# Two of the four down products of each slab of the last MLP, by seven block products in place of eight

## The chip, the cores and the metric

One core of one Trainium2 chip runs the whole program; the metric is its device time in microseconds (us), as the median of three runs. The engines are TensorE (PE in the profile; PEld is its weight load), VectorE (DVE), ScalarE (ACT), GpSimd (POOL) and SyncE (SP), which here only issues DMAs. A difference of about 0.2% of this kernel's time is what a measurement can tell from no change.

## What is computed

A network of four layers on 256 tokens of width 2048, in float32. Only the last part matters here: the second MLP of the second block, and the norm ahead of it and behind it.

```
def sqrelu_mlp(h, w1, w2):
    a = jax.nn.relu(h @ w1)          # 256x2048 @ 2048x8192
    return (a * a) @ w2              # 256x8192 @ 8192x2048

# second_block, last layer (i = 1)
x = x + mix
x = x + sqrelu_mlp(rmsnorm(x, norm_mlp[1]), mlp_w1[1], mlp_w2[1])
return rmsnorm(x, norm_final)
```

Every float32 matrix product is made of three products of a rounded type (fp32r): with a = ah + al and w = wh + wl it is ah·wh + ah·wl + al·wh, summed in PSUM. So each weight is loaded from HBM once, and split on the chip into a high part (a rounding copy) and a low part (the difference).

## The kernel before

**Weights.** SP loads chunks of 512x512 weights (1 MB) into RAW, which has four slots (`NR = 4`, line 18); `load(c)` waits until the chunk that held the slot has been split. A chunk has two halves of 1024 elements a partition. A half is what the rings hold: `split_next` on ACT writes the high part to WH, `split_next` on DVE writes the low part to WL (RAW minus WH), each ring with four places (`RS = 4`). I call a half **a unit**. ACT and DVE run the same loop: during unit n of TensorE they split unit n + 3, and ACT may write its place once TensorE has read unit n - 1.

**The second MLP** (`mlp(1, ...)`, the function `mlp` of each engine) goes over 8 slabs of 1024 hidden columns. One turn of its loop does, for slab s and the slab before: up product `m1u{s}0`, up product `m1u{s}1`, then the four down products `m1d{s-1}0` to `m1d{s-1}3`, each 512 output columns wide. An up product is 8 units: 16 blocks of 128 rows, four column blocks, three matmuls each, 192 matmuls that move 256 columns (tokens) past a 128x128 weight block. A down product is 4 units: 8 blocks of rows, two blocks of tokens, three matmuls each, 48 matmuls that move 512 columns (weights) past a 128x128 block of tokens. Eight slabs have 32 down products.

Behind each up product and each of its two PSUM banks, ACT takes the relu to RE, DVE multiplies relu by relu into SQ, ACT makes the high part Bh and DVE the low part Bl. Behind each down product DVE adds the two banks, times the squared norm factor of the token, to X (`accumulate`). GpSimd has nothing to do in this MLP; its work ends with the layer before.

**The end.** The last down product `m1d73` goes token block by token block (`gemm_by_tokens`), so that the norm of the first 128 tokens runs beside the matmuls of the second; then come the final norm and the stores.

**Names.** G are the four PSUM banks of the products, T the other four; A3h and A3l are the normed input of the MLP, high and low; RB holds the norm factor of each token along a row.

## Time and profile before

| | |
|---|---|
| device time, median of 3 runs | 2880.29 us (2875.42 to 2881.31) |
| span of the profiled execution | 2881.1 us |
| PE busy in the span | 2841.2 us (99%) |
| one turn of the second MLP, 2305.35 to 2392.41 | 87.06 us |
| DVE / ACT busy in it | 49.4 / 38.2 us |
| GpSimd busy in it | 0 us |

The profile is of one execution. A matmul row's duration is the time until its result is out, some 0.28 to 0.39 us, and rows overlap; what a matmul costs TensorE is the distance from start to start. In a timeline a row is the start, the duration, engine, line, operation, out<-in, and behind it in brackets the idle time of the engine ahead of it and what ended that. The chain view gives start, length and work of each piece of the chain that ended last. In a table of windows each engine's busy time stands with its number of instructions, then the granted TensorE clock, the DMA share and GB/s.

### The profile page before, as it was taken

What the parts mean: (1) busy time and instruction counts of PE and PEld (TensorE: products, weight loads), DVE (VectorE), ACT (ScalarE), POOL (GpSimd) and SP (SyncE); (2) the same over time, 40 slices, a digit from 0 to 9 for tenths busy, and PEclk for the clock granted to TensorE, in tenths of its full rate; (3) what the DMA queues carried; (4) which work ended last, traced back from release to release, by engine and by line L of the source; (5) the groups of instructions that cost most, each with busy time, mean ns of one, the idle gap of its engine ahead of it and who ended that gap; (6) DMA issues with size and microseconds to landing.
All of it is one profiled execution on the core that took longest, in us unless ns stands there. A gap on an engine that the chain in (4) does not pass through costs nothing.

```text
span 2881.1 us, 46128 instructions
## 1 busy us (share of the span) xinstructions
PE 2841.2 (99%) x19454; PEld 2585.9 (90%) x19454; DVE 1848.5 (64%) x2543; ACT 1408.0 (49%) x1980; POOL 374.1 (13%) x420
## 2 busy tenths in 40 slices
PE   8999999999999999999999999989999999999998
PEld 8999988998899998999998899878889899988997
DVE  6998655776576665677665666677555555555555
ACT  5434645556555555444444445654545444444444
POOL 0000000000000000007883654122000000000000
PEclk9999999999999999999999999999999999999999
DMA  7555455552555555567776666586655555555553
GB/s 243 191 190 174 137 201 182 190 188 88 175 188 171 171 174 176 191 203 241 237 239 214 237 234 210 200 248 194 199 191 190 194 197 194 190 190 196 197 192 132
DMA packets 288047, 557.99 MB, mean 194 GB/s; under 512 B 25376, under 2 KB 35872, under 8 KB 287584
## 3 DMA queue, kind: packets, MB, share of 16 engines
q1 hardware_dynamic: 275328, 514.49, 54.3%
q0 software_dynamic: 5600, 22.78, 2.0%
q10 hardware_dynamic: 6912, 17.76, 1.8%
q8 instruction: 154, 2.52, 0.4%
q14 instruction: 53, 0.43, 0.0%
HBM read 530.87 MB, written 24.12 MB: 193 GB/s over the span
## 4 chain that ended last, share of the span: by engine, by line
PE 91%; DVE 4%; ACT 2%; DMA 1%; issue 1%; SPq 0%; ACTq 0%; POOL 0%; DVEq 0%
PE G L506 86%; PE T L506 3%; DVE WL L1714 1%; ACT WH L1103 1%; DVE Y L1722 1%; DMA FD<-s_k 1%; PE T L585 1%; DMA s_k<-VAR 1%; DVE XX L1714 0%; PE G L983 0%; ACT L1100 0%; ACT SC_e L1106 0%; DVE ZZ L2374 0%; DVE ST L1795 0%; DVE SC_e L1722 0%
## 5 line engine op out<-in xcount | busy, mean ns | idle before, releaser
L1714 DVE TENSOR_TENSOR WL<-RAW,WH 128x1024 fp32r<-128x1024 f32 (+1 forms) x948 | 1183.1, 1256 | 766.3 <-ACT WH L1103 756.6
L1103 ACT ACTIVATE WH<-RAW 128x1024 fp32r<-128x1024 f32 (+1 forms) x948 | 994.7, 1056 | 1027.7 <-PE G L506 1026.5
L506 PE MATMUL G<-A1h,WH 128*128 128x256 f32 (+1 forms) x2587 | 720.4, 280 | 3.1 <-DVE WL L1714 2.1
L506 PE MATMUL G<-A1l,WH 128*128 128x256 f32 x2560 | 712.9, 278 | 0.0
L506 PE MATMUL G<-A1h,WL 128*128 128x256 f32 x2560 | 711.5, 278 | 0.0
L506 PEld LDWEIGHTS G<-A1h,WH 128*128 128x128 f32 x2587 | 487.3, 189 | 7.0 <-DVE WL L1714 3.1
L506 PEld LDWEIGHTS G<-A1l,WH 128*128 128x128 f32 x2560 | 483.9, 189 | 0.4
L506 PEld LDWEIGHTS G<-A1h,WL 128*128 128x128 f32 x2560 | 482.9, 189 | 0.0
L506 PE MATMUL G<-WH,Bh 128*128 128x512 f32 x1024 | 399.3, 390 | 0.6 <-DVE WL L1714 0.6
L506 PE MATMUL G<-WH,Bl 128*128 128x512 f32 x1024 | 398.5, 389 | 0.0
L506 PE MATMUL G<-WL,Bh 128*128 128x512 f32 x1024 | 398.5, 389 | 0.0
L506 PE MATMUL G<-A3h,WH 128*128 128x256 f32 (+1 forms) x1033 | 283.4, 276 | 0.0
L506 PE MATMUL G<-A3l,WH 128*128 128x256 f32 x1024 | 283.2, 277 | 0.0
L506 PE MATMUL G<-A3h,WL 128*128 128x256 f32 x1024 | 282.7, 276 | 0.0
L506 PEld LDWEIGHTS G<-WH,Bh 128*128 128x128 f32 x1024 | 192.3, 188 | 40.2 <-DVE WL L1714 1.0
L506 PEld LDWEIGHTS G<-WH,Bl 128*128 128x128 f32 x1024 | 192.2, 188 | 40.1
L506 PEld LDWEIGHTS G<-WL,Bh 128*128 128x128 f32 x1024 | 192.3, 188 | 39.0
L506 PE MATMUL G<-WH,A1h 128*128 128x512 f32 (+1 forms) x512 | 203.2, 397 | 0.4 <-DVE WL L1714 0.4
L506 PE MATMUL G<-WH,A1l 128*128 128x512 f32 (+1 forms) x512 | 198.9, 388 | 0.0
L506 PE MATMUL G<-WL,A1h 128*128 128x512 f32 (+1 forms) x512 | 197.6, 386 | 0.0
L506 PEld LDWEIGHTS G<-A3h,WH 128*128 128x128 f32 x1033 | 193.7, 188 | 0.6
L506 PEld LDWEIGHTS G<-A3h,WL 128*128 128x128 f32 x1024 | 192.3, 188 | 0.0
(332 smaller groups left out, 3461.5 us busy)
## 6 DMA issues: line engine op xcount, KB each, us to landing
RAW<-in_mlp_w SPq DMA_DIRECT2D x256, 1024.0 KB, 5.3
RAW<-in_even_w_in SPq DMA_DIRECT2D x52, 1024.0 KB, 5.1
RAW<-in_a_w_in SPq DMA_DIRECT2D x48, 1024.0 KB, 5.2
RAW<-in_b_w_glu SPq DMA_DIRECT2D x32, 1024.0 KB, 5.2
RAW<-in_odd_w_in SPq DMA_DIRECT2D x20, 1024.0 KB, 5.1
RAW<-in_even_w_out SPq DMA_DIRECT2D x16, 1024.0 KB, 5.0
RAW<-in_odd_w_out SPq DMA_DIRECT2D x16, 1024.0 KB, 5.0
RAW<-in_a_w_out SPq DMA_DIRECT2D x16, 1024.0 KB, 5.0
```

The lines of the kernel that those rows point to most:

```text
L506: return e.matmul(out, lhsT, rhs, start=start, stop=stop, skip_group_check=True)
L585: m = e.transpose(T[:, 256 * j + 128 * i:256 * j + 128 * i + 128], X[:, i, c:c + 128], IDENT)
L1103: return e.activation(out, in_, ACT.Copy, scale=scale, bias=0.0)
L1714: return e.tensor_tensor(out, a, b, op)
L1722: return e.scalar_tensor_tensor(out=out, in0=a, scalar=s, in1=b, op0=op0, op1=op1)
```

## The change

**Two of the four down products of a slab** (`SEVEN = (0, 2)`: output columns 0 to 511 and 1024 to 1535) become seven block products. The tokens fall into two halves of 128, the 1024 rows of the slab into two of 512, the 512 columns into two of 256. Eight products of such blocks are the plain way; seven products of sums of blocks give the same. One block product is 4 row blocks by 3 matmuls, 12 matmuls that move 256 columns, and is a unit of the rings: 1024 elements a partition, like a half before. So such a down product has 7 units where it had 4.

**Weight sums on GpSimd:** four adds of 128x1024 for each such down product, S2 = b21 + b22, S1 = b12 + b22, S3 = S1 + b21, S4 = S3 + b11, from the two RAW chunks to TSUM. **Token sums on GpSimd:** four adds of 128x512 a slab, HS to TSUM (named DSUM there). ACT and DVE split them as they split the raw blocks, and the token sums once more to DH and DL.

**The way of the activations:** DVE takes relu times the norm factor to RM in one instruction, ACT squares it to HS; the split of HS to EH and EL, and of the sums to DH and DL, comes as one 128x1024 instruction at each of the first four units of the next up product (`second_highs`, `second_lows`). For the last slab it comes in `m1d62` and `m1d63`. RE, SQ, Bh and Bl fall away. **The sums of products:** seven PSUM halves T are added to ACC in SBUF over all slabs by DVE, and at the end eleven instructions of 128x256 for each of the two turn ACC into X (`add_blocks`). **The order:** up 0, down 0, down 1, up 1, down 2, down 3. **Memory:** the ring's places are 1152 wide for this MLP, WL and others lie elsewhere, GR2 is loaded at the last turn. The norm factor's row RB is made by two more small matmuls in `m1u00`.

The table of the products, and TensorE's part:

```
+SEVEN = (0, 2)
+PRODUCTS = ("21*11", "22*21", "D4*12", "D1*S2", "D2*S1", "D3*S3", "11*S4")
...
+            for q, p in enumerate(PRODUCTS):
+                n = next(half)
+                if q % 2 == 0 and before is not None:
+                    e.wait_ge(*q_acc[before, q // 2])
+                e.wait_ge(*w_lo[n])
+                hi, lo = slot((WH, WHm), n), slot((WL, WLm), n)
+                Ah, Al = blocks(p)
+                o = TB[q // 2][:, 256 * (q % 2):256 * (q % 2) + 256]
+                for j in range(4):
+                    mm(o, Ah[:, j, :], hi[:, j, :], j == 0 and q % 2 == 0, False)
+                    mm(o, Ah[:, j, :], lo[:, j, :], False, False)
+                    m = mm(o, Al[:, j, :], hi[:, j, :], False, j == 3)
+                m.then_inc(*w_read.up(n))
+                step(STEPS[tag])
```

VectorE's part of a down product of seven:

```
+            for h, p in enumerate(PRODUCTS):
+                n = next(half)
+                while split[0] < min(n + RS, limit[0]):
+                    split_next()
+                if h in (2, 4, 6) and not first:
+                    add_products(tag, k, h // 2 - 1)
+                step(STEPS[tag])
+            if not first:
+                add_products(tag, k, 3)
+            if sums:
+                add_blocks(tag, k)
```

GpSimd's weight sums:

```
+            for i in range(2):
+                e.wait_ge(*w_in[(c + i) % NR][c + i])
+            if before is None:
+                e.wait_ge(*x_up["gg3", 1])
+            else:
+                e.wait_ge(*w_lo[product(before, "D2*S1")])
+            tt(S2, b21, b22, ALU.add).then_inc(*t_sum.up((tag, 0)))
+            tt(S1, b12, b22, ALU.add).then_inc(*t_sum.up((tag, 1)))
+            if before is not None:
+                e.wait_ge(*w_lo[product(before, "11*S4")])
+            e.wait_ge(*d_l[s, 1])
+            e.wait_ge(*t_sum[tag, 1])
+            tt(S3, S1, b21, ALU.add).then_inc(*t_sum.up((tag, 2)))
+            e.wait_ge(*t_sum[tag, 2])
+            tt(S4, S3, b11, ALU.add).then_inc(*t_sum.up((tag, 3)))
```

SyncE's wait ahead of a load, for the chunk that held the slot:

```
                 old = c - NR
-                e.wait_ge(*w_lo[half_of[old, 1]])
+                first = old if old in tag_of else old - 1
+                if chunks[old][2]:
+                    tag = tag_of[first]
+                    e.wait_ge(*w_lo[product(tag, "D4*12" if old == first else "22*21")])
+                    e.wait_ge(*t_sum[tag, 3 if old == first else 2])
```

The order of the instructions shows three places. First VectorE, from the first unit of an up product to the end of the down products behind it. Before (an up product's last eight splits, the activations, the first splits of the next product):

```order
L1714 TENSOR_TENSOR WL<-RAW,WH 128x1024 [waits s_w_hi] x8
L1722 SCALAR_TENSOR_TENSOR SQ<-G,RE 128x512 [waits s_m_l,s_m_relu]
L1714 TENSOR_TENSOR Bl<-SQ,Bh 128x512 [waits s_m_h]
L1722 SCALAR_TENSOR_TENSOR SQ<-G,RE 128x512 [waits s_m_l,s_m_relu]
L1714 TENSOR_TENSOR Bl<-SQ,Bh 128x512 [waits s_m_h]
```

Now, for `m1u{s}0` and the product of seven behind it:

```order
L1891 TENSOR_TENSOR WLm<-RAW,WHm 128x1024 [waits s_w_hi]
L1891 TENSOR_TENSOR EL<-HS,EH 128x1024 [waits s_m_h]
L1891 TENSOR_TENSOR WLm<-RAW,WHm 128x1024 [waits s_w_hi]
L1891 TENSOR_TENSOR EL<-HS,EH 128x1024 [waits s_m_h]
L1891 TENSOR_TENSOR WLm<-RAW,WHm 128x1024 [waits s_w_hi]
L1891 TENSOR_TENSOR DL<-TSUM,DH 128x1024 [waits s_d_h]
L1891 TENSOR_TENSOR WLm<-RAW,WHm 128x1024 [waits s_w_hi]
L1891 TENSOR_TENSOR DL<-TSUM,DH 128x1024 [waits s_d_h]
L1891 TENSOR_TENSOR WLm<-RAW,WHm 128x1024 [waits s_w_hi] x4
L1899 SCALAR_TENSOR_TENSOR RM<-G,RB 128x512 [waits s_m_sq,s_bank0]
L1899 SCALAR_TENSOR_TENSOR RM<-G,RB 128x512 [waits s_m_sq,s_w_read]
L1891 TENSOR_TENSOR WLm<-TSUM,WHm 128x1024 [waits s_w_hi] x3
```

Four splits of activations stand among the weights' splits of the up product, and the two RM stand ahead of the split of the fourth block product (the first of the three with TSUM). Second ScalarE at that boundary, now:

```order
L1217 ACTIVATE HS<-RM 128x512 [waits s_d_sum,s_m_l,s_ev_d] x2
L1220 ACTIVATE WHm<-TSUM 128x1024 [waits s_w_read,s_t_sum]
L1220 ACTIVATE EH<-HS 128x1024 [waits s_m_sq,s_w_read]
L1220 ACTIVATE WHm<-TSUM 128x1024 [waits s_w_read,s_t_sum]
L1220 ACTIVATE EH<-HS 128x1024 [waits s_m_sq]
```

The two squares stand ahead of the high part of the fourth block product; here, in `m1d62`, the activations' splits stand among the products too. Third GpSimd, one slab of the MLP, where it had nothing:

```order
L2731 TENSOR_TENSOR TSUM<-HS 128x512 [waits s_w_lo,s_m_sq]
L2731 TENSOR_TENSOR TSUM<-HS 128x512
L2731 TENSOR_TENSOR TSUM<-TSUM,HS 128x512 [waits s_d_sum]
L2731 TENSOR_TENSOR TSUM<-TSUM,HS 128x512 [waits s_p_sum]
L2731 TENSOR_TENSOR TSUM<-RAW 128x1024 [waits s_w_lo,s_w_in3,s_w_in2]
L2731 TENSOR_TENSOR TSUM<-RAW 128x1024
L2731 TENSOR_TENSOR TSUM<-TSUM,RAW 128x1024 [waits s_t_sum,s_d_l,s_w_lo]
L2731 TENSOR_TENSOR TSUM<-TSUM,RAW 128x1024 [waits s_t_sum]
```

Token sums come first, then the four weight sums, the first of which waits for both chunks of the down product and the third for the low part of the token sums; the second down product has the last four rows again.

## Rows read from the trace of the kernel before

**Rows 1.** The page's first part: busy us (share) xinstructions.

```profile
PE 2841.2 (99%) x19454; PEld 2585.9 (90%) x19454; DVE 1848.5 (64%) x2543; ACT 1408.0 (49%) x1980; POOL 374.1 (13%) x420
```

**Rows 2.** Windows: a turn, an up product, a down product.

```profile
2305.35:2392.41 87.06, 87.06 (x578) 79.60 (x577) 49.37 (x49) 38.24 (x40) 0.00 (x0) 1.00 0.58 193
2305.35:2327.12 21.77, 21.77 (x194) 21.77 (x193) 10.98 (x10) 8.87 (x9) 0.00 (x0) 1.00 0.59 191
2348.88:2359.76 10.88, 10.88 (x51) 9.03 (x50) 7.42 (x9) 6.00 (x8) 0.00 (x0) 1.00 0.51 177
```

**Rows 3.** Timeline of PE: an up product's first row.

```profile
2305.35 0.33 PE L506 MATMUL G<-A3h,WH 128*128 128x128 f32 x2
```

**Rows 4.** Timeline of ACT in that turn; columns as above.

```profile
2305.55 1.06 ACT L1103 ACTIVATE WH<-RAW 128x1024 fp32r<-128x1024 f32 x1 [1.60 <-PE G L506]
2308.45 1.06 ACT L1103 ACTIVATE WH<-RAW 128x1024 fp32r<-128x1024 f32 x1 [1.83 <-PE G L506]
2328.64 0.58 ACT L1100 ACTIVATE RE<-G 128x512 f32<-128x512 f32 x1
2330.63 2.00 ACT L1103 ACTIVATE WH<-RAW 128x1024 fp32r<-128x1024 f32 x2
```

**Rows 5.** Timeline of DVE in that turn.

```profile
2306.64 1.23 DVE L1714 TENSOR_TENSOR WL<-RAW,WH 128x1024 fp32r<-128x1024 f32 x1
2329.38 0.68 DVE L1722 SCALAR_TENSOR_TENSOR SQ<-G,RE 128x512 f32<-128x512 f32 x1
2331.71 3.50 DVE L1714 TENSOR_TENSOR WL<-RAW,WH 128x1024 fp32r<-128x1024 f32 x3 [0.26 <-ACT WH L1103]
2359.66 1.41 DVE L1722 SCALAR_TENSOR_TENSOR X<-G,NS,X 128x512 f32<-128x512 f32 x2
```

**Rows 6.** DMA issues: out<-in, engine, count, KB each, median us to landing.

```profile
RAW<-in_mlp_w SPq DMA_DIRECT2D x256, 1024.0 KB, 5.3
```

**Rows 7.** Timelines of POOL and DVE around two long GpSimd operations.

```profile
1762.28 1.91 POOL L2471 TENSOR_TENSOR TC<-CV,ST 128x1024 f32<-128x1024 f32 x1 [3.29 <-issue]
1763.68 1.59 DVE L1714 TENSOR_TENSOR WL<-RAW,WH 128x1024 fp32r<-128x1024 f32 x1 [1.44 <-ACT WH L1103]
1764.14 2.88 POOL L2471 TENSOR_TENSOR TC<-CV,ST 128x1024 f32<-128x1024 f32 x1
...
1779.42 2.39 POOL L2471 TENSOR_TENSOR TS<-TC,TS 128x1024 f32<-128x1024 f32 x1 [7.23 <-ACT TS L1556]
1780.33 2.57 DVE L1714 TENSOR_TENSOR WL<-RAW,WH 128x1024 fp32r<-128x1024 f32 x1 [1.77 <-ACT WH L1103]
```

**Rows 8.** The same where both engines have work queued, 1355 to 1360.

```profile
1355.87 1.66 DVE L1714 TENSOR_TENSOR WL<-RAW,WH 128x1024 fp32r<-128x1024 f32 x1
1356.41 1.62 POOL L2471 TENSOR_TENSOR TS<-TS,LAM 128x256 f32<-128x256 f32 x1
1357.46 1.66 DVE L1714 TENSOR_TENSOR WL<-RAW,WH 128x1024 fp32r<-128x1024 f32 x1
1358.00 1.62 POOL L2471 TENSOR_TENSOR TS<-TS,LAM 128x256 f32<-128x256 f32 x1
```

**Rows 9.** GpSimd's line 2471, duration ns min/median/max.

```profile
L2471 POOL TENSOR_TENSOR TS<-TC,TS x4: 2393/2399/2409, 1779.4 to 1836.5; 128x1024 f32<-128x1024 f32 x4
L2471 POOL TENSOR_TENSOR VAR<-VAR,CV x1: 1050/1050/1050, 1757.9 to 1757.9; 128x512 f32<-128x512 f32 x1
```

**Rows 10.** Timeline of PE behind a wait, and the window of it.

```profile
339.41 0.89 PE L506 MATMUL T<-SC_e,V 128*128 128x256 f32 x4 [1.93 <-ACT SC_e L1103]
341.17 0.41 PE L506 MATMUL G<-A1h,WH 128*128 128x256 f32 x1
341.38 0.41 PE L506 MATMUL G<-A1l,WH 128*128 128x256 f32 x1
340.00:344.00 4.00, 4.00 (x23) 4.00 (x22) 2.75 (x4) 3.36 (x7) 0.00 (x0) 0.57 0.79 262
```

**Rows 11.** Timeline of DVE: the last product's second half of tokens.

```profile
2872.11 0.75 DVE L1722 SCALAR_TENSOR_TENSOR X<-G,NS,X 128x512 f32<-128x512 f32 x1 [1.10 <-PE G L506]
```

More of the change, by code:

```diff
@@ L280, in build_program, with weights @@
     turn = itertools.cycle((0, 2))
-    def weights(tag, w, K, n0, N=512, fm=False, first=0, steps=0, split=True):
+    def weights(tag, w, K, n0, N=512, fm=False, first=0, steps=0, seven=False):
         kts = K // 128
@@ L524, in gemm @@
                     end = seen == kts
-                    hi, lo = WH[:, n % RS, j * N:(j + 1) * N], WL[:, n % RS, j * N:(j + 1) * N]
+                    hi, lo = (slot(ring, n)[:, j * N:(j + 1) * N] for ring in ((WH, WHm), (WL, WLm)))
                     if fm:
@@ L568, in gemm_by_tokens @@
                         e.wait_ge(*w_lo[n])
-                    hi, lo = WH[:, n % RS, j * N:(j + 1) * N], WL[:, n % RS, j * N:(j + 1) * N]
+                    hi, lo = (slot(ring, n)[:, j * N:(j + 1) * N] for ring in ((WH, WHm), (WL, WLm)))
                     mm(o, Ah[:, kt, tk], hi, kt == 0, False)
@@ L1732, in split_next, with gemm @@
             c, h = halves[n]
[L1733 to L1734 removed]
+            if h in PRODUCTS:
+                src = seven_source(tag_of[c], h)
+            else:
+                N = chunks[c][1][1]
+                src = RAW[:, c % NR, h * 2 * N:(h + 1) * 2 * N]
             e.wait_ge(*w_hi[n])
[L1736 to L1739 removed]
+            tt(slot((WL, WLm), n), src, slot((WH, WHm), n).bitcast(F32), ALU.subtract).then_inc(*w_lo.up(n))
+        def gemm(tag, soon=None, at=2):
+            for h in range(units(tag)):
                 n = next(half)
@@ L2218, in dve, with first_mlp @@
         norm_scale("m0", 3)
-        def mlp(l, ph, Ah, Al, gains, after=None):
-            Bh, Bl, RE, SQ = MLP[l]
+        def first_mlp():
             for s in range(9):
@@ new lines, in first_mlp, with second_lows @@
+            finish()
+            norm_scale("s", 3)
+        def second_lows(s):
+            at = s // 7
+            for k in range(2):
+                e.wait_ge(*m_h[1, s, k])
+                low(EL[at][:, 4 * k:4 * k + 4, :], HS[:, 4 * k:4 * k + 4, :], EH[at][:, 4 * k:4 * k + 4, :]).then_inc(
+                    *m_l.up((1, s, k)))
+                yield
+            if at:
+                for _ in range(units("m1d62") - 2):
+                    yield
+            for k in range(2):
+                e.wait_ge(*d_h[s, k])
+                low(DL[at][:, 2 * k:2 * k + 2, :], TSUM[2 + k][:, :].rearrange("p (a b) -> p a b", b=512),
+                    DH[at][:, 2 * k:2 * k + 2, :]).then_inc(*d_l.up((s, k)))
+                yield
```

419 lines of the change are left out of this document (318 added, 101 removed).

## The prediction

> **What bounds the kernel now.** I read the engines' busy time first: TensorE is busy 2841.2 of the span [rows 1]. The windows of one turn of the second MLP come next: TensorE is busy in all of its 87.06 us at a granted clock of 1.00, and VectorE, ScalarE and GpSimd are busy 49.4, 38.2 and 0 us [rows 2]. So what the matmuls cost sets the time, and the other engines matter only where they come too late. The profiled execution's span is 2881.1 us, 0.8 above the median of 2880.29; I work from the span and take the 0.8 off at the end.
>
> How late they may come is in the timelines. An up product starts at 2305.35 [rows 3]. Behind the boundary of a unit ScalarE starts the high part 0.20 later, and 2308.45 is 0.38 behind the next boundary (2305.35 + 2.72); I take 0.33 inside an up product [rows 4]. It takes 1.06, VectorE's low part starts 1.09 after it and takes 1.23 [rows 4, 5]. So a unit's low part is there 2.5 us after the boundary that freed its place, and TensorE wants it three units after that boundary. With units of 2.72 us this is 8.2, a spare of 5.6.
>
> **What the change takes off TensorE.** An up product moves 256 columns in 192 matmuls in 21.77 us, 0.1134 each, with a new weight block each time; a down product moves 512 columns in 48 in 10.88, 0.2267 each [rows 2]. Seven block products are 84 matmuls of 256 columns: 84 x 0.1134 = 9.53. Each replaced product saves 10.88 - 9.53 = 1.36, sixteen save 21.7. The two matmuls for RB cost TensorE about 0.3, by their like of 128 columns.
>
> **What it does to the spare time.** A unit in a product of seven is 12 x 0.1134 = 1.36 us, so three units are 4.08 and the spare is 1.5. And behind an up product it is less. Let 0 be the boundary. VectorE makes RM of the second bank once it is complete (0.33), 0.68 long, 0.69 apart [rows 5]; its end is at about 1.1. ScalarE squares it, 0.58 [rows 4], to 1.7, and only then makes the high part of the fourth block product, for the squares stand ahead of it in its queue: 1.68 to 2.74. VectorE's low part ends at 4.0, and TensorE wants it at 4.08. **The spare of the fourth block product is nil**, and each us by which VectorE comes late to that boundary is a us of waiting. The next ones have little: VectorE needs 1.14 for a split back to back [rows 5] and about 0.71 for each PSUM addition, which the two X of 1.41 show [rows 5], together 2.98 for two products of 2.72; with that the seventh comes just in time (within 0.1). So without GpSimd fourteen of the sixteen pay nothing.
>
> **What GpSimd's sums do to VectorE.** The trace has GpSimd and VectorE's splits side by side, and they shut each other out. GpSimd's 128x1024 addition of two arrays begins at 1779.42 and ends at 1781.81; VectorE's split begins at 1780.33 and takes 2.57 in place of 1.23, that is 1.49 of waiting and 1.08 of work [rows 7]. The other way, GpSimd's second of 1764.14 waits for the split that ends at 1765.27 and takes 2.88, where the first, alone, takes 1.91 [rows 7]. With work queued on both they take turns: splits at 1355.87 and 1357.46 of 1.66, GpSimd's at 1356.41 and 1358.00 [rows 8]. The weight sums read two arrays from SBUF: the nearest rows are the four of 2.39 to 2.41 [rows 9]; the lower bound is the 1.91 of the one with constants along rows. I take 2.40, 2.27 of it behind a turn, and 1.08 for each split. The token sums, 128x512, lie between the 1.05 [rows 9] and half of 2.40; I take 1.15.
>
> When do they run? Both chunks must have landed. The second one's slot comes free with the first split in the up product, at 2.5, and a load lands 5.3 later [rows 6]: 7.9 from the up product's start. Every such group of sums thus runs in the up product ahead of its own down product.
>
> In `m1u{s}1` (for the third down product), from the up product's start: sums and splits in turn, 8.07 + 4 x 2.27 + 4 x 1.08 = 21.5 for the fourth sum and the seventh split (the splits come due every 2.72, at 9.6 to 17.7, so that one always waits), then the eighth split to 22.65. Undisturbed it ends at 2.72 x 7 + 1.45 + 1.23 = 21.7. RM of bank 0 follows to 23.3, of bank 1 to 23.9; the square to 24.5; high part to 25.5; low part to 26.7. TensorE wants it at 21.77 + 4.08 = 25.85. **It waits 0.95.**
>
> In `m1u{s}0` (for the first) the splits DL0 and DL1 stand in the same stretch. From 8.07 seven splits (DL0, DL1 and five of weights) and four sums have the path in turn without a gap: 8.07 + 7 x 1.08 + 4 x 2.27 = 24.7, and 25.0 with the starts between. The second block product's low part is at 23.9 where TensorE wants it at 23.13: 0.77; then RM, square, high and low part as above bring the fourth to 29.05, where it is wanted at 26.62: 2.45. **It waits 3.2.** That is more than the 1.36 saved.
>
> The sum: saved 21.7. Waits: six turns of 3.2 for the first and seven of 0.95 for the third, 19.2 + 6.7. In the second turn of the loop the token sums come late (slab 0 has no down products before it), into the up product itself: twenty uses in turn by VectorE and GpSimd instead of eleven; the same working gives 7 in place of 3.2. `m1d62` has the splits EL0 and EL1 between its own products, on VectorE 2 x 1.14 against no spare: 2.2. `m1d70` has no up product ahead; its token sums, DL splits and weight sums all fall into `m1d62` and `m1d63`, 12.7 + 10.9 us, with the third and fourth sum at about 17 and 20 after the start of `m1d63`: three of its units late by 2 to 2.5 each, 6.5 (bounds 0 and 8). `m1d72` 0.5, an estimate between nothing and 1, since its chunks are loaded only once the fourth sum of `m1d70` is done. The tail: `add_blocks` and the gains hold VectorE in `m1d73` until the first half of tokens is some 2 us old, which moves the start of the last chain [rows 11] by 1. With RB 0.3: 19.2 + 6.7 + 7 + 2.2 + 6.5 + 0.5 + 1 + 0.3 = 43.4. **43.4 - 21.7 = 21.7 slower**: span 2902.8, time 2902.0.
>
> What costs nothing by this sum: the three ring places 1152 wide (the first unit waits for one more read, spare 5.6); the loads, which carry as much as before, 0.58 of the DMA share [rows 2]; GR2, 1 MB at the last turn; ACC's first copies on ScalarE. If GR2 delays a load, 1 us.
>
> The Trainium skill, GPSIMD Engine Reference, section 2.1 on instruction dispatch, gives a two-input addition a floor of about 2.5 cycles an element, at 1.2 GHz an estimate of 2.13 us for 1024. The row has 2.40 and decides; with 2.13 each group of four would end 1.1 earlier, and the sum would be some 15 lower. The same skill, SBUF — State Buffer, section Who interferes with whom, says that a VectorE instruction with two SBUF inputs and a GpSimd instruction that reads SBUF exclude each other for a whole instruction; the trace agrees (2.57 for 1.23). By that page the splits are the wrong neighbours for sums on GpSimd, which speaks against this change.
>
> **Rivals.** *Faster: the splits keep their pace.* If VectorE, whose next split is already queued, gets the path ahead of the waiting sum, the fourth sum slides behind the last splits, under RM and the squares, which read PSUM or run on ScalarE. Then only `m1d62`, part of `m1d70`, the tail and RB stay, 2.2 + 1 + 0.3 up to 6: 2880.3 - 21.7 + 3.5 to 6 = 2862 to 2865. The rows of 1355 to 1358 speak against it: there GpSimd gets its turn each time. It decides where the eighth split ends: before 21.8 after the up product's start this rival holds, from there on each us counts. Chance 0.23.
>
> *No change: the sums are shorter.* With 1.91 for a sum [rows 7] each group ends 1.9 earlier: 1.3 in the first and 0 in the third, 5 in the early one, 4.5 in `m1d70`: 7.8 + 5 + 2.2 + 4.5 + 1.8 = 21.3 against 21.7, 2880. Between this and the forecast lies 2875 to 2892. Chance 0.17. For it: the one row of 1.91; against: four rows of 2.39 and more.
>
> *Slower still: the clock falls.* After a wait of 1.93 the window 340 to 344 shows a granted clock of 0.57, part of it at 1.2 GHz, and matmuls of 256 columns 0.21 apart in place of 0.113; behind 340.5 there are 15 of them, which costs 1.5 us [rows 10]. Waits of 0.77 and 2.45 in each first product are as long. If the clock falls there eight times, 8 x 1.5 = 12 more, 2914; if the stretch is twice as long each time, 2926. Chance 0.2.
>
> *It doesn't do what it says:* seven products cost TensorE as much as eight, since stationary blocks of tokens change twice as often per column. The up products show 0.1134 with a change at each matmul, so 0.02; time as forecast plus up to 21.
>
> **The numbers.** The forecast, 2892 to 2910, has 0.38. Its time is 2902. With 0.23 for 2862 to 2865, 0.17 for 2875 to 2892, 0.2 for 2910 to 2926 and 0.02 beyond, the range 2862 to 2918 holds about 0.85. The unknown prices lie in it: `m1d70` at 0 is 2895, a token sum of 1.2 adds 1. Faster by over 0.2% (5.8 us, about what a measurement of this kernel tells from no change) means below 2874.5: 0.24. Within it, up to 2886: 0.11. Slower: 0.65.
>
> **What would show it.** TensorE's row for T<-WHm,EH: in a window of undisturbed block products 0.1134 from start to start, or the saving is wrong. GpSimd's TSUM<-RAW 2.4 us or more, and up to 3.5 where it waits. WLm<-RAW in up products with medians well above 1.23, up to 2.6 to 3.5; if they stay at 1.23 in the second half of an up product, the rival is right. TensorE's idle time before T<-WHm,DH (the fourth product, D1*S2, is the second with DH), released by VectorE WLm, about 2.5 behind each first and 1 behind each third. PEclk below 1.00 in the slices of the last third speaks for the falling clock. Wrong would be the forecast if the second chunk lands before 5 or after 11 us of the up product, since then the sums meet other splits.

## The result and the profile after

| | before | changed |
|---|---|---|
| median of the runs shown, us | 2880.57 (2875.42 to 2881.31) | 2923.28 (2917.97 to 2929.21) |
| span of the profiled execution | 2881.1 | 2920.4 |
| ratio, 95% interval | | 1.0158 (1.0141 to 1.0174) |
| start of the second MLP to the end of the last matmul, profiled execution | 698.8 | 745.1 |

The changed kernel is 42.7 us slower by the two medians, and some 45 by the ratio. The forecast was 21.7 slower: the direction holds, the size is half of what came, and 2923 lies above the range. The first part of the page of the changed kernel answers to [rows 1]: TensorE is busy 9 us less, VectorE 217 us more and GpSimd 273 us more.

```profile
PE 2832.1 (97%) x20041; PEld 2598.7 (89%) x20041; DVE 2065.9 (71%) x2640; ACT 1469.9 (50%) x2036; POOL 647.2 (22%) x516
```

**A steady turn.** Windows of the changed kernel from one first up product's start to the next, and from the start of `m1d70` to the last matmul (us, then the busy time of PE, PEld, DVE, ACT and POOL with instructions, the granted clock, the DMA share and GB/s). Here the turn is 88.75 (the five steady ones 88.75 to 89.03). Before it was 87.17 from start to start; the window of 87.06 in [rows 2] stops 0.11 short of the next up product. And TensorE is no longer busy in all of the turn:

```profile
2396.46:2485.21 88.75, 85.42 (x651) 81.06 (x650) 75.72 (x59) 45.74 (x46) 33.87 (x12) 1.00 0.57 190
...
2842.50:2911.10 68.60, 49.47 (x267) 42.15 (x265) 61.21 (x73) 25.63 (x36) 21.09 (x8) 0.88 0.23 83
```

The chain that makes the first product wait, in the turn that starts at 2396.46: timelines of POOL, DVE, ACT and PE (start, duration, engine, line, operation, out<-in, count, and in brackets the idle time before it and who ended it).

```profile
2404.09 6.14 POOL L2731 TENSOR_TENSOR TSUM<-RAW 128x1024 f32<-128x1024 f32 x2 [11.38 <-issue]
2412.58 6.60 POOL L2731 TENSOR_TENSOR TSUM<-TSUM,RAW 128x1024 f32<-128x1024 f32 x2 [2.35 <-DVE DL L1891]
...
2404.45 3.48 DVE L1891 TENSOR_TENSOR DL<-TSUM,DH 128x1024 fp32r<-128x1024 f32 x1
2407.85 3.46 DVE L1891 TENSOR_TENSOR WLm<-RAW,WHm 128x1024 fp32r<-128x1024 f32 x1
2411.24 1.21 DVE L1891 TENSOR_TENSOR DL<-TSUM,DH 128x1024 fp32r<-128x1024 f32 x1
2412.37 9.03 DVE L1891 TENSOR_TENSOR WLm<-RAW,WHm 128x1024 fp32r<-128x1024 f32 x4
2421.32 1.27 DVE L1899 SCALAR_TENSOR_TENSOR RM<-G,RB 128x512 f32<-128x512 f32 x2
...
2422.03 1.23 ACT L1217 ACTIVATE HS<-RM 128x512 f32<-128x512 f32 x2 [5.09 <-DVE RM L1899]
2423.17 3.89 ACT L1220 ACTIVATE WHm<-TSUM 128x1024 fp32r<-128x1024 f32 x4
...
2420.32 0.38 PE L577 MATMUL T<-WHm,EH 128*128 128x256 f32 x1 [0.46 <-DVE WLm L1891]
...
2425.52 0.38 PE L577 MATMUL T<-WHm,DH 128*128 128x256 f32 x1 [2.21 <-DVE WLm L1891]
...
2468.74 0.39 PE L577 MATMUL T<-WHm,DH 128*128 128x256 f32 x1 [0.66 <-DVE WLm L1891]
```

The sums over the whole MLP (duration min, median, max in ns):

```profile
L2731 POOL TENSOR_TENSOR TSUM<-RAW x32: 2461/3423/3552, 2222.9 to 2865.3; 128x1024 f32<-128x1024 f32 x32
```

The timelines read as the prediction's working goes: the second chunk has landed 7.6 us after the start of the up product, the first sum begins there, a split beside a sum takes 3.4 to 3.5 in place of 1.23, RM of the second bank follows late, behind it the squares, and behind them the high part of the fourth block product. The second block product waits 0.46, the fourth 2.21, and the third down product waits 0.66, at its fourth block product too. Over the whole second MLP a split of a raw block takes 1697 ns in the mean, against the 1.23 of [rows 5] (group of the page: busy, mean ns, idle before):

```profile
L1891 DVE TENSOR_TENSOR WLm<-RAW,WHm 128x1024 fp32r<-128x1024 f32 x240 | 401.3, 1697 | 96.9 <-ACT WHm L1220 96.8
```

**The end.** The last 68.6 us, the four down products `m1d70` to `m1d73`, hold 41 us of matmuls. The timelines of DVE, POOL and PE there, first m1d70, then m1d71, then the second `add_blocks` in m1d73, and last a window that begins within m1d71's wait:

```profile
2843.83 3.44 DVE L1891 TENSOR_TENSOR DL<-TSUM,DH 128x1024 fp32r<-128x1024 f32 x1
...
2847.37 0.36 PE L577 MATMUL T<-WHm,EH 128*128 128x256 f32 x1 [4.29 <-DVE DL L1891]
...
2855.12 0.39 PE L577 MATMUL T<-WHm,DH 128*128 128x256 f32 x1 [1.63 <-DVE WLm L1891]
...
2861.82 6.13 POOL L2731 TENSOR_TENSOR TSUM<-RAW 128x1024 f32<-128x1024 f32 x2 [7.84 <-DMA RAW<-in_mlp_w]
2868.12 4.84 POOL L2731 TENSOR_TENSOR TSUM<-TSUM,RAW 128x1024 f32<-128x1024 f32 x2 [0.17 <-POOL TSUM L2731]
...
2863.00 1.00 DVE L1891 TENSOR_TENSOR ACC<-ACC,T 128x512 f32<-128x512 f32 x2
2864.04 10.46 DVE L1891 TENSOR_TENSOR ACC<-ACC 128x256 f32<-128x256 f32 x7
2874.54 1.43 DVE L1891 TENSOR_TENSOR X<-X,ACC 128x256 f32<-128x256 f32 x4
2875.89 1.22 DVE L1891 TENSOR_TENSOR WLm<-RAW,WHm 128x1024 fp32r<-128x1024 f32 x1
...
2877.16 0.79 PE L577 MATMUL G<-WHm,EH 128*128 128x512 f32 x1 [7.95 <-DVE WLm L1891]
...
2896.90 2.81 DVE L1891 TENSOR_TENSOR ACC<-ACC 128x256 f32<-128x256 f32 x7
...
2872.00:2882.40 10.40, 5.24 (x12) 4.13 (x13) 9.02 (x14) 4.18 (x7) 0.96 (x1) 0.51 0.30 102
```

`add_blocks` for the first product stands on VectorE ahead of the split of m1d71's fourth unit. It takes 11.9 us where the second time, with GpSimd idle, it takes 4.2 (2.81 and 1.43): its first seven additions take turns with the four sums for m1d72. The split that TensorE wants at 2869.2 ends at 2877.1, a wait of 7.95. In m1d73 it is the same place and 4.46 us. The granted clock fell to 0.5, the lower of the two levels, 3.0 us into m1d71's wait and stayed there for 10.2 us.

The wait of 4.29 is not one of the late weight sums: it stands ahead of the first matmul of m1d70, since TensorE waits there for DL, the low part of the token sums, which VectorE makes last (the first row). The token sums themselves began only at 2830.61, once the last split of m1d62 was done.

**Where the 46.4 us of the MLP lie.** I took the distance from each matmul's start to the next. Of it 0.1134 or 0.2267 is the work; the rest is a *wait* where the next one had over 0.1 idle before it, *low clock* where the granted clock was 0.5, and otherwise *small*.

| us | before | changed | difference |
|---|---|---|---|
| work | 696.8 | 675.3 | -21.4 |
| waits | 0 | 54.1 | +54.1 |
| low clock | 0 | 7.3 | +7.3 |
| small | 1.5 | 8.0 | +6.6 |
| sum | 698.3 | 744.7 | +46.6 (46.4 by the edges; some records are missing) |

The waits by stretch: 9.1 up to the end of the first two turns (2307.5), 3.8 in each of the five steady turns, 5.8 in the turn from 2751.8 with m1d62's splits, 20.1 behind it.

In the pair of profiled executions the changed kernel reaches the second MLP 7.4 us earlier, 2165.9 against 2173.3. That can't be put down to the change: the changed kernel and the twelve below that have its places in memory start the second MLP at 2160.6 to 2173.8. In the window 120 to 250 its matmuls lie closer, 952 weight loads to 917, but a later kernel with the same places in memory up to there shows 917 too:

```profile
120.00:250.00 130.00, 130.00 (x918) 121.49 (x917) 128.09 (x231) 51.57 (x51) 0.00 (x0) 1.00 0.58 189
...
120.00:250.00 130.00, 130.00 (x954) 122.12 (x952) 130.00 (x237) 52.55 (x52) 0.00 (x0) 1.00 0.60 195
...
120.00:250.00 130.00, 130.00 (x918) 121.50 (x917) 128.08 (x231) 51.57 (x51) 0.00 (x0) 1.00 0.58 189
```

(Before; changed; the kernel `e5_short` below.) So profiled executions of the same places differ there, and the medians, 42.7 apart, say more than the profiled spans, 39.3 apart.

### The profile page after: what moved, and what is told of

The parts are those of the page before. It is cut to its first block, busy times and chain, and to the rows that moved or that the text cites. A ratio compares the mean times of both kernels' runs of the same rounds, so it can differ in the third digit from the quotient of the medians.

```text
span 2920.4 us, 47703 instructions
## 1 busy us (share of the span) xinstructions
PE 2832.1 (97%) x20041; PEld 2598.7 (89%) x20041; DVE 2065.9 (71%) x2640; ACT 1469.9 (50%) x2036; POOL 647.2 (22%) x516
## 4 chain that ended last, share of the span: by engine, by line
PE 79%; DVE 13%; ACT 4%; issue 2%; DMA 1%; SPq 0%; ACTq 0%; POOL 0%; DVEq 0%
PE G L577 72%; DVE WLm L1891 6%; PE T L577 6%; DVE WL L1891 1%; DVE DL L1891 1%; ACT WHm L1220 1%; ACT WH L1220 1%; DVE Y L1899 1%; DVE ACC L1891 1%; PE T L683 1%; DMA FD<-s_k 1%; DMA s_k<-VAR 1%; DVE RM L1899 1%; DVE X L1891 0%; DVE XX L1891 0%
## 5 line engine op out<-in xcount | busy, mean ns | idle before, releaser
L1891 DVE TENSOR_TENSOR WL<-RAW,WH 128x1024 fp32r<-128x1024 f32 (+1 forms) x692 | 873.5, 1270 | 494.9 <-ACT WH L1220 488.9
L1220 ACT ACTIVATE WH<-RAW 128x1024 fp32r<-128x1024 f32 (+1 forms) x692 | 725.1, 1054 | 681.3 <-PE G L577 679.2
L1891 DVE TENSOR_TENSOR WLm<-RAW,WHm 128x1024 fp32r<-128x1024 f32 x240 | 401.3, 1697 | 96.9 <-ACT WHm L1220 96.8
L1220 ACT ACTIVATE WHm<-RAW 128x1024 fp32r<-128x1024 f32 x240 | 254.3, 1062 | 269.1 <-PE G L577 247.1
L577 PE MATMUL G<-A3h,WHm 128*128 128x256 f32 (+1 forms) x1040 | 284.2, 276 | 3.6 <-DVE WLm L1891 3.6
L577 PE MATMUL G<-A3l,WHm 128*128 128x256 f32 x1024 | 283.7, 277 | 0.0
L577 PE MATMUL G<-A3h,WLm 128*128 128x256 f32 x1024 | 282.9, 276 | 0.0
L577 PE MATMUL G<-WH,Bh 128*128 128x512 f32 x512 | 200.1, 391 | 0.6 <-DVE WL L1891 0.6
L577 PE MATMUL G<-WH,Bl 128*128 128x512 f32 x512 | 199.4, 389 | 0.0
L577 PE MATMUL G<-WL,Bh 128*128 128x512 f32 x512 | 199.3, 389 | 0.0
```

What stands on the lines that cost most here:

```text
L577: return e.matmul(out, lhsT, rhs, start=start, stop=stop, skip_group_check=True)
L1220: return e.activation(out, in_, ACT.Copy, scale=scale, bias=0.0)
L1891: return e.tensor_tensor(out, a, b, op)
```

## Experiments

Each is compared with the kernel before on the same chip, and the ratios are to that. The experiments ran on five chips, where the kernel before had medians of 2876.5 to 2879.8, so a difference of a few us between two medians of this table is not sure; where two kernels are compared by a few us, I give the ratios too.

| kernel | median us | ratio, 95% |
|---|---|---|
| changed | 2923.3 | 1.0158 (1.0141 to 1.0174) |
| e1_memset: no weight sums | 2874.0 | 0.9988 (0.9976 to 1.0) |
| e2_end: X formed later | 2924.5 | 1.0157 (1.0141 to 1.0174) |
| e3_swap: plain product first | 2909.5 | 1.0098 (1.0078 to 1.0119) |
| e4_layout: before, X and WL moved | 2905.8 | 1.0096 (1.0081 to 1.0111) |
| e5_short: third product alone, plain end | 2878.5 | 1.0001 (0.9991 to 1.0011) |
| e6_noblocks: X not formed | 2914.0 | 1.0118 (1.0103 to 1.0133) |
| e7_lastfree: no sums for slab 7 | 2913.2 | 1.0111 (1.0093 to 1.0128) |
| e8_pad: e4 and a pad | 2877.1 | 1.0 (0.9986 to 1.0013) |
| e9_fifth: fifth place | 2919.0 | 1.0139 (1.0115 to 1.0162) |
| e10_fifth_short: and plain end | 2896.6 | 1.0061 (1.0045 to 1.0078) |
| e11_fifth_third: and third alone | 2875.0 | 0.9991 (0.9977 to 1.0005) |
| **e12_fifth_swap**: e10, plain product first | **2864.7** | **0.9952 (0.9932 to 0.9971)** |
| e13_swap_short: e12, four places | 2886.8 | 1.0036 (1.0023 to 1.0049) |
| e14_full_end: e12, changed kernel's end | 2889.8 | 1.0049 (1.0031 to 1.0067) |

**1. Are the sums the cost at all?** Each weight sum becomes three memsets, so GpSimd is busy about as long as an undisturbed sum (2.5 us) and starts at the same landing, but reads nothing. The kernel leaves out the weight sums: four of the seven weight operands are zeros.

```
-            tt(S2, b21, b22, ALU.add).then_inc(*t_sum.up((tag, 0)))
+            filled(0).then_inc(*t_sum.up((tag, 0)))       # the same for S1, S3, S4
```

> The changed kernel, but GpSimd's four weight sums of each product of seven are replaced by three memsets each (128x1024, 128x1024, 128x512) into the same buffer: some 2.5 us that write SBUF and read nothing. The token sums stay. It leaves out the weight sums, so four of the seven products are of zeros. Theory A (a sum that reads SBUF and a split on VectorE shut each other out): WLm<-RAW takes 1.2 us throughout, TensorE's waits of 3.0 us in the first and 0.8 us in the third down product of each turn vanish (under 0.2), a turn takes 84.3 + 0.7 = 85.1 us, the wait of 4.3 ahead of m1d70 falls below 1, and the whole is 2923 - 6x3.8 - 5 - 4 - 3 (add_blocks no longer in turn with sums) - 4 (low clock) = about 2884. Theory B (VectorE and ScalarE have too much to do for units of 1.36 us, or the sums come too late as data): the waits stay at 3 and 0.8, the whole within 5 us of 2923.

A turn without a wait, at 84.64, beside memsets on GpSimd at 2389.36, 7.6 us behind the turn's start, as the sums were:

```profile
2381.72:2466.36 84.64, 84.64 (x651) 80.87 (x650) 61.40 (x59) 45.72 (x46) 28.07 (x28) 1.00 0.60 199
...
2389.36 1.97 POOL L2875 MEMSET TSUM<- 128x1024 f32 x2 [11.15 <-issue]
```

The whole loss is gone, 49 us, and the time is 10 us below the 2884 that I had expected. What is left against the kernel before, 3.7 us, can't be told from no change: of the 21.7 saved, 13.1 go into waits (m1d73's 4.50 the longest), 2.8 into the low clock and 3.3 into more small gaps. Since the landing and the length are kept, lateness alone does not make the waits: the shutting-out of VectorE does. That the zeros let TensorE run faster is out as a rival for the turns, since the granted clock is 1.00 in a steady turn of either kernel. The Trainium skill, SBUF — State Buffer, section Who interferes with whom, calls the ports that VectorE and GpSimd share an exclusive lock, and has a VectorE instruction with two SBUF inputs contend with a GpSimd instruction that reads SBUF, and not with one that only writes it; the 3.46 beside a sum and the 1.22 beside a memset agree.

**2. The end.** First the eleven additions of `add_blocks` moved behind the next units' splits, in two pieces:

```
             if sums:
-                add_blocks(tag, k)
+                beside(add_blocks(tag, k))
```

> The changed kernel, but the eleven instructions of add_blocks no longer stand ahead of the split of the fourth unit of the next product (m1d71, m1d73): they run in two pieces behind the first two units' splits there, and ScalarE's squares of that block two units later. Theory A (TensorE's waits of 7.95 and 4.46 us in the last two plain products are for the split queued behind add_blocks): both waits fall below 1, of the 5.75 us lost at 1.2 GHz behind 2842 some 4 go too, the whole is 2923 - 12 - 4 = about 2907. Theory B (they are for the loads, or for the turns with GpSimd's sums, which remain): at most 4 us less.

No gain where I had expected 16 us: that theory of the cure fell, and the time is in Theory B's range. m1d71 and m1d73 no longer wait, but m1d72 does, four times, its splits now behind the second piece and the sums. The first of them, 0.74, 0.96 and 1.79 follow:

```profile
2882.65 0.55 PE L577 MATMUL T<-WHm,EH 128*128 128x256 f32 x1 [4.09 <-DVE WLm L1893]
```

Then, each alone: nine of the eleven additions left out (`e6_noblocks`), and memsets for the sums of slab 7 only (`e7_lastfree`).

```
-            (nine additions on ACC and X in add_blocks)
             tt(x[0][1], x[0][1], q["D2*S1"], ALU.add)     # this and the one for x[1][1] stay
```

> The changed kernel with nine of the eleven operations of add_blocks left out (X gets two of the products in place of their combination, so columns 0 to 511 and 1024 to 1535 of it are not what is asked). It prices what I had priced at 1 us. Theory A (the forming of X in turn with GpSimd's sums holds back the split of the 4th unit of m1d71 and m1d73): the waits of 7.95 and 4.46 us go, and with them two stretches at the low clock: 2904 to 2911. Rival B (the wait only moves, since the sums of m1d72 are late anyway): waits of 4 us and more appear in m1d72, 2915 to 2921.

```
-            tt(S2, b21, b22, ALU.add)
+            (tt(S2, b21, b22, ALU.add) if s < 7 else filled(0))     # the same for S1, S3, S4
```

> The changed kernel with real sums of weights for slabs 0 to 6, and memsets in their place for slab 7 alone (its fourteen products use zeros for four of seven weight operands). Theory A: the steady turns stay at 88.8; in the last turn the waits of 4.29, 1.63 and 7.95 us shrink to under 1 each, those of m1d73 (4.5) stay as in the kernel without any sums: 2905 to 2912. Rival B (the last turn is held by the forming of X alone, whatever the sums do): the wait of m1d71 stays at 5 us or more, 2915 to 2921.

The first gives 9.3 us by the medians and 11.5 by the ratios, the second 10.1 and 13.5. Waits of m1d71 and m1d73, first without the additions, then without the sums:

```profile
2873.00 0.68 PE L577 MATMUL G<-WHm,EH 128*128 128x512 f32 x1 [2.39 <-DVE WLm L1891]
...
2895.51 0.50 PE L577 MATMUL G<-WHm,EH 128*128 128x512 f32 x1 [0.96 <-DVE WLm L1891]
```

```profile
2870.02 0.50 PE L577 MATMUL G<-WHm,EH 128*128 128x512 f32 x1 [0.47 <-DVE WLm L1891]
...
2895.23 0.50 PE L577 MATMUL G<-WHm,EH 128*128 128x512 f32 x1 [4.48 <-DVE WLm L1891]
```

The 7.95 at m1d71 needs both, the additions ahead of the split and the sums beside them, and 2.39 of it stays without the additions; the 4.5 at m1d73 needs the additions alone. Both times lie 1 to 3 us above what Theory A gave. The two savings are of one wait in the main and can't be added up.

**3. The steady turn.** The plain m1d{s}1 ahead of the first product of seven:

```
+    def downs(s, nb):
+        return (1, 0) if nb == 0 and s < 8 else (2 * nb, 2 * nb + 1)
```

> The changed kernel, but in each turn up to s = 7 the plain down product m1d{s}1 comes ahead of m1d{s}0 of seven, so that a plain one stands behind the first up product. Theory A (the wait is there because behind an up product the fourth block product has no spare time): a plain product has units of 2.72 us and takes up the lateness; the waits of 3.0 us a turn fall to 0 to 1.2, the whole is 14 to 20 us less, 2903 to 2909. Theory B (VectorE and GpSimd together lack throughput around a product of seven, wherever it stands): the waits move with it and stay at 2.5 to 3.5 a turn, the whole within 4 us of 2923.

14 us less by the medians, 17 by the ratios. m1d{s}0 has no wait in the steady turns, but the third down product waits longer than before the swap: 1.53 to 1.76 in five turns, and 2.36 and 2.11 in the two behind which the clock fell. So a part of the wait moved, which Theory A had at 1.2 at most. A turn without the low clock is 86.98:

```profile
2393.25:2480.23 86.98, 85.25 (x652) 81.28 (x651) 73.84 (x59) 45.95 (x46) 32.59 (x12) 1.00 0.56 189
...
2463.77 0.39 PE L581 MATMUL T<-WHm,DH 128*128 128x256 f32 x1 [1.73 <-DVE WLm L1895]
```

Then a fifth place for a landed chunk, in memory that is free in the second MLP, and nothing else:

```
+    RAW5 = sb("RAW5", [128, 2048], ctx=ctx)
+    def place(c):
+        i = (c - FIFTH) % 5
+        return c % NR if c < FIFTH else (FIFTH + i - 1) % NR if i else 4
```

> The changed kernel with a fifth place for a landed chunk, from m1u01 on, in memory that is free there; nothing else is changed, so each chunk's load can start 5.4 us earlier. Theory A (the first product's 3.2 us and the third's 0.8 us come from the second chunk's landing, behind which GpSimd's sums begin): both waits are under 0.5 us, a turn falls from 88.8 to 84.9 to 85.5 us, the last turn's waits of 4.3 and 7.95 us shrink too, since the sums of m1d70 begin earlier; 2885 to 2896. Rival B (the sums are held by something else: their places in TSUM, VectorE's token splits, the turns taken with VectorE): the waits stay, 2918 to 2925. Rival C (the transfers themselves are the limit, 16 of some 5 us in a turn): the turn falls to 86 to 87.5 only.

The median moved by 4 us only, which the intervals can't tell from nothing, and my 2885 to 2896 was wrong. The waits of 0.66 in the third product and of 0.46 in the first went, the 2.2 stayed. POOL, DVE, ACT and PE in the turn from 2300.93, and the windows of it, of the next turn and of 3.4 us behind the wait:

```profile
2304.68 5.85 POOL L2741 TENSOR_TENSOR TSUM<-RAW 128x1024 f32<-128x1024 f32 x2 [7.86 <-issue]
2316.28 6.60 POOL L2741 TENSOR_TENSOR TSUM<-TSUM,RAW 128x1024 f32<-128x1024 f32 x2 [5.76 <-DVE DL L1901]
...
2316.08 9.03 DVE L1901 TENSOR_TENSOR WLm<-RAW,WHm 128x1024 fp32r<-128x1024 f32 x4
2325.03 1.27 DVE L1909 SCALAR_TENSOR_TENSOR RM<-G,RB 128x512 f32<-128x512 f32 x2
...
2300.93:2389.63 88.70, 86.52 (x652) 82.57 (x651) 75.20 (x59) 45.73 (x46) 33.46 (x12) 0.98 0.56 189
2389.63:2476.89 87.26, 85.06 (x652) 81.03 (x651) 75.53 (x59) 45.72 (x46) 33.33 (x12) 1.00 0.58 193
2329.00:2332.40 3.40, 3.17 (x15) 3.17 (x16) 3.40 (x5) 1.90 (x3) 0.00 (x0) 0.50 0.99 371
```

S2 and S1 now begin 3.8 us into the turn. But S3 waits 5.76 us for DL, since the token sums lie in the same TSUM, so S3 and S4 again meet the last splits of the up product, RM begins only 2.2 us behind the up product's end, and the fourth block product is late with it. And with that single wait the clock falls in five of the six turns that have it, at 1.4 us each (88.70 against 87.26): what the earlier landing gave, the clock took. With a plain last turn besides (slab 7 by eight products, X formed in pieces in m1d63 and m1d70):

```
-   ... seven=k in SEVEN)
+   ... seven=k in SEVEN and s < 8)
```

> The fifth place, and slab 7 taken as in the kernel before (eight block products for all four down products, no sums of weights or tokens), with X formed in pieces beside the units of m1d63 and m1d70. Theory A: seven turns of 85.2 in place of 87.06 (13 us less), the ring change 1.4 and the early waits 2 us more, no wait in the last turns: 2865 to 2872, below the kernel before by 0.2 to 0.4%. Rival B (waits stay at 3.2 and 0.8 a turn): 2886 to 2892.

The end's 22 us came, the turn's not: 88.75 with the wait and one low clock in each of six turns. Both of my expectations were too low, Theory A by 25 us and Rival B, which had no low clock, by 5. The third product alone, first with four places, then with five:

```
-SEVEN = (0, 2)
+SEVEN = (2,)
```

> Seven block products for one down product per slab (the third) in place of two, and for slabs 0 to 6 only: the last turn is the plain one of the kernel before, and the eleven operations that form X from the products stand in pieces beside the units of m1d63 and m1d70. Theory A (what costs is the first product's late sums and the end, where sums and the forming of X hold VectorE's splits up): a steady turn is 84.3 + 1.36 (the saving given up) + 0.8 (the third's wait) + 0.4 of small ones = 86.9 us against 87.06 of before, no wait over 1.5 us in the last turns and no low clock in them; with the 7 us by which the kernels with the changed places reach the second MLP earlier: 2867 to 2876 us, below both kernels. Rival B (the block form costs by itself: small gaps between products, the ring change, the memory places): 2880 to 2890.

> Seven block products for the third down product alone, slabs 0 to 6, slab 7 plain, and the fifth place for a landed chunk. Theory A (in the third product the wait of 0.7 us is the landing's alone, and no sum reaches back into an up product's last splits): no wait in a steady turn, no low clock, a turn of 85.7 + 0.3 to 0.5 = 86.0 to 86.2 us; against the kernel before 7 us less, the ring change 1.4 and slab 0 about 1 more: 2872 to 2877. Rival B (the sums slow VectorE's splits wherever they stand): waits of 0.7 us stay and the clock falls once a turn as with both products: 2879 to 2885.

With four places the turn was 86.93 in three of five, as worked out, and 87.1 and 87.5 in the others; the waits of 0.7 remained, and the time is that of the kernel before, 2 us above my range (the 7 us of an earlier start did not come, see above). With five no wait is left in a steady turn, which is 85.97, but 0.9991 can't be told from no change.

**4. Both causes together.** Order, fifth place and plain end:

> The fifth place and the plain last turn as before, seven block products for the first and the third, the plain m1d{s}1 ahead of m1d{s}0. With the fifth place and the old order one wait of 2.2 us is left in each turn, behind splits of 3.4 us that GpSimd's S3 and S4 held up, and the clock falls behind it. Theory A (with a plain product between, VectorE has caught up when the first sum is asked for): that wait is under 1 us and the clock stays, a turn of 84.9 to 85.8 us: 2866 to 2874, below the kernel before. Rival B (the held-up splits let the plain product wait in its place, or the third one): 2 us of waits a turn and the low clock stay, 2885 to 2897.

A steady turn has no wait, and the end none beyond 0.7 (windows of a turn and of the last 66 us):

```profile
2378.48:2463.46 84.98, 84.98 (x651) 81.22 (x650) 72.60 (x59) 45.84 (x46) 33.22 (x12) 1.00 0.59 198
2783.20:2849.50 66.30, 64.80 (x324) 54.57 (x322) 53.06 (x79) 33.88 (x45) 0.00 (x0) 1.00 0.37 128
```

The turn is 2.2 us under the 87.17 of the kernel before, and the kernel is 0.5% under the one before: it beats both. Its two neighbours divide the loss:

> The kernel of the best run so far without the fifth place for a landed chunk: plain m1d{s}1 ahead of m1d{s}0, slab 7 plain, four places. Theory A (both causes count: the late landing of the second chunk, and the held-up splits behind the up product): the waits of the swapped order stay at 1.5 to 1.8 us and the turn at 86.9, as when only the order was swapped; the plain end saves 29 us against that run: 2876 to 2883. Rival B (with a plain end the order alone is enough): turn 85 to 85.6, 2864 to 2870.

> The kernel of the best run so far with the changed kernel's own end: slab 7 by seven block products too, its sums on GpSimd and add_blocks in one piece. It prices the end by itself, on turns without waits. Theory A (the end's loss does not hang on the turns before it: splits queued behind add_blocks and behind slab 7's sums, then the low clock): waits of 4 to 8 us at m1d70, m1d71 and m1d73 as in the changed kernel, 25 to 35 us above the 2864.7 of the plain end: 2890 to 2900. Rival B (the fifth place lets the sums of slab 7 begin early enough): half of it or less, 2868 to 2880.

Four places instead of five cost 0.8% of the time, 24 us (1.0036 against 0.9952), and the time lies 4 us above Theory A. In the profiled pair the MLP is 18.8 us longer: the wait of 1.6 to 2.2 is back in seven turns, 14.7 us of waits in all, the clock fell twice, 3.0, and small gaps are 1.0 more; the rest up to 24 no trace shows. The changed kernel's end costs 1.0%, 28 us, on turns that don't wait: as Theory A had it (25 us by the medians). The last stretch, from the last up product's end to the last matmul, is 90.90 against 66.30 above, at a clock of 0.89:

```profile
2796.40:2887.30 90.90, 70.89 (x396) 60.58 (x395) 81.12 (x91) 41.55 (x53) 33.77 (x12) 0.89 0.29 98
...
2877.74 0.80 PE L591 MATMUL G<-WHm,EH 128*128 128x512 f32 x1 [4.50 <-DVE WLm L1905]
```

**5. The places in memory.** The kernel before with X and WL (and what lies between) where the changed kernel has them:

```
     RAW = sb("RAW", [128, NR, 2048])
+    X = sb("X", [128, 2, D])
...
     RB = sb("RB", [128, 256])
+    sb("pad_wl", [128, 16])
+    (WL, RD2 and places_wl moved here from above X)
```

> The kernel before, with only the places in SBUF changed as the changed kernel has them (X ahead of the rings, WL behind RB). In the changed kernel's profile the matmuls of 120 to 250 us are 0.1135 us apart where before had 0.118, and the first 350 us are 5 to 7 us shorter. Theory A (the places do it): 0.1135 there, 4 to 7 us less than before. Theory B (one execution differs from another there): no difference in the times beyond 1 us.

I had put this at nothing or a gain; it cost 28 us. The turn is 90.97 where it was 87.17: matmuls of 256 columns come 0.120 apart in place of 0.1134 in the second MLP. Three rows of PE, and a window of 90.6 us, busy throughout and at a clock of 1.00:

```profile
2420.09 0.28 PE L503 MATMUL G<-A3h,WL 128*128 128x256 f32 x1
2420.21 0.28 PE L503 MATMUL G<-A3h,WH 128*128 128x256 f32 x1
2420.33 0.28 PE L503 MATMUL G<-A3l,WH 128*128 128x256 f32 x1
...
2393.20:2483.80 90.60, 90.60 (x577) 81.98 (x576) 49.30 (x49) 38.21 (x40) 0.00 (x0) 1.00 0.55 185
```

In that kernel A3h begins 4096 words a partition behind the start of WL, exactly the ring's length. But the down products don't read A3h, and their matmuls of 512 columns are slower too, 0.2334 in the mean in place of 0.2267. One line more:

```
+    sb("pad_a3", [128, 112], ctx=ctx)
     A3h = sb("A3h", [128, 16, 256], F32R, ctx)
```

> The kernel before with the changed kernel's places for X and WL, as in the layout run, and 112 words in front of the third MLP operand's buffers A3h and A3l. Theory P (the pitch of the matmuls hangs on how far the stationary operand lies from the moving one): the pitch in the second MLP returns from 0.120/0.235 to 0.1135/0.227 us, the earlier stages keep 0.1135: 2868 to 2874, below the kernel before. Rival Q (the place of X or WL alone sets it): pitch 0.120 stays, 2903 to 2908.

The pitch is 0.1134 again, a turn 87.17, and the ratio 1.0. So the places matter, and the changed kernel's own, with 512 and 112 words ahead of A3h, have the pitch of 0.1134. Why they matter is open: the pad moves all that lies behind it, A3l and the down products' operands too, and no run tells them apart. That the time fell below the kernel before, as I expected, did not come. This kernel's profiled execution has 0.118 in the window 120 to 250 and that of `e4_layout` 0.1135, with the same places up to there, so that difference belongs to the execution.

## Why the prediction was off

In the column measured, a wait's cost is the distance between two starts beyond the work, with the idle time in brackets; the rows from m1d70 to `add_blocks` give idle time.

| step | forecast us | measured us |
|---|---|---|
| taken off TensorE | -21.7 | -21.4 |
| first product's wait, a steady turn | 3.2 | 3.0 (0.46 and 2.21 idle) |
| third product's wait | 0.95 | 0.8 (0.66 idle) |
| the second turn's first product | 7 | 6.6 |
| in m1u00, ring change and RB | 0 | 1.6 (1.42 idle) |
| m1d62, with its share of the third's | 2.2 + 0.95 | 2.8 |
| m1d70 | 6.5 | 5.9 (4.29 and 1.63) |
| m1d72 | 0.5 | 0.8 |
| add_blocks: m1d71 and m1d73 | 1, in the tail | 12.4 (7.95 and 4.46), tail 0.3 |
| low clock | a rival | 7.3 |
| small gaps, RB among them | 0.3 | 6.6 |

**Right:** the mechanism and its size in the turns, which `e1_memset` and `e12_fifth_swap` bear out. The nil spare of the fourth block product, the two uses in turn of one path, the stretch in which the sums run, and the place of the two waits came as the prediction has them; a steady turn was put at 4.15 of waits less 2.72 saved, +1.43, and the waits were 3.8. (For m1d70 the size is right by luck: 6.5 was three late units in the middle of it, and what came is a wait of 4.29 at its head for the token sums' low part and one of 1.63.) The matmuls cost what was said, so the last rival is out. The rival of a VectorE that keeps its pace is out too: the sums get their turn each time (a median of 3.42, against the 2.40 of [rows 9] and 2.46 for the shortest one), and so is that of shorter sums. By the Trainium skill, GPSIMD Engine Reference, section 2.1, such a sum has a floor of about 2.5 cycles an element, at 1.2 GHz an estimate of 2.13 us; the shortest here took 2.46, so the trace agrees.

**Wrong, first: the step on the tail.** It priced `add_blocks` by what it does to the last chain [rows 11], 1 us, and did not ask what is queued behind it on VectorE. A split that TensorE wants three units later stands behind all eleven instructions, twice; and for m1d70's, GpSimd's sums for m1d72 run at that moment, so 4.2 us become 11.9. The order of the changed kernel's instructions shows that place without any trace: in m1d71 the split of the fourth unit comes behind `add_blocks`. Runs e6, e7 and e14 show the price: 9.3 us less without the additions, 10.1 without the sums beside them, and 28 for the whole end, the waits of m1d70 and the low clock with it.

**Wrong, second: the clock was a rival and not a term.** The prediction put it behind the first product's waits. In the changed kernel it did not fall there in any steady turn. It fell once in the second turn (3.4 us from 2247.54, a cost of 1.5) and three times with the longer waits at the end, 5.8 us in all. With one wait left in the turn (e9, e10) it did fall in eleven of twelve turns, 1.4 us each time, about the price that [rows 10] gave. So price and kind were right and the place was not in the main; what decides between the turn with two waits and that with one stays open.

**Wrong, third: nothing for small gaps.** A turn has 0.6 to 0.8 us of them where before it had 0.1. Without the sums 0.3 is left (84.64 against 87.06 less 2.72), so half of it goes with the sums; the best kernel has 0.65. I can't name what each gap waits for, they are under 0.1.

**Missed besides:** in m1u00, 11 us into the MLP, a unit waits 1.42 for its split. Every kernel with the new ring and RB has that wait, the kernel with only the places of the changed one (e4) has none. The prediction gave the ring change a spare of 5.6 and asked only after the split itself. The traces show what stands behind it: ScalarE's third split into the new ring waits for one more read and starts 0.26 us into the MLP, where before it started 2.50 us ahead of it, and the last instructions of the layer before and those of the norm stand behind it on ScalarE, and on VectorE behind that unit's low part. VectorE comes to the splits that follow the norm 9.81 us into the MLP, before at 7.06. Of these 2.75 the ring change makes 2.35, and the two instructions on DG for RB 0.4.

The sum, without the 1 us in the tail: the forecast was 20.7 for the MLP and 46.4 came. `add_blocks` 12.4, the clock 7.3, small gaps 6.3, m1u00 1.6, about 1 at the end between an idle time and the distance of starts, 0.3 less saved, and 3.2 less in the other waits: 25.7. The medians leave 21 of it, the ratio 24.

The places in memory, which have no term in the prediction, do cost nothing in the changed kernel as far as the runs tell, since its matmuls are 0.1134 apart; by e4 it could have been 28 us.

## What to carry to other kernels

Fewer matmuls pay only if the engines that feed them keep pace at the new, shorter unit, and work handed to GpSimd is not free of VectorE's time when both read two arrays from SBUF: each shuts the other out for a whole instruction (a split of 1.23 us took 3.46 here), so place such work where VectorE has a spare of several us, or let another stage stand between it and the instruction that is wanted next (plain product first and one more place for a landed chunk; with a plain end too it is 58.6 us less than the changed kernel, for a saving kept in seven slabs of eight). At the end of a pipeline ask of each block of instructions what stands behind it on its queue, not only what it does to the last chain. And price a wait of some us at the end of a dense stretch with the stretch at the low clock behind it.

## What the runs showed of the hardware

- The pitch of matmuls depends on where tensors lie in SBUF: 0.120 against 0.1134 us for 256 columns by a move of 112 words (e4, e8), 28 us in this kernel, with no wait and a clock of 1.00. Which tensor it is stays open.
- It also differs between executions (917 or 952 weight loads in the window 120 to 250, with the same places in memory up to there), and the start of the second MLP lies between 2160 and 2180 in the profiled ones.
- GpSimd's memset does not shut out VectorE's split: 1.22 beside it. GpSimd's addition does: VectorE's split takes up to 3.5 beside it, and the addition itself 2.46 at the least and 3.42 in the median.
- The granted clock fell to 0.50 for 3.4 us with a single wait of 1.9 to 2.2 us in eleven of twelve turns (e9, e10). With a pair of 0.46 and 2.2 us, 5 us apart, it fell in 2 of 24 turns (none of six in the changed kernel, one of six in e2 and in e6, none in e7).
